# A hybrid decoder layer on 8 cores: query heads transposed in pairs, the convolution's projection ahead of the output transposes, and another order of the first transfers

## What is computed

```python
x = x + 0.5 * swiglu(rmsnorm(x, ffn1_norm), ffn1_w_gate, ffn1_w_up, ffn1_w_down)   # 1024 -> 2816 -> 1024
h = rmsnorm(x, mix_norm)
proj = h @ w_in            # q_lat 384 | kv_lat 256 | k_rope 32 | xc, gB, gC 1024 each | two gates 1024 each
q = (rmsnorm(q_lat, q_a_norm) @ w_uq).reshape(b, s, 8, 96)     # 64 plain dims, 32 rotary dims per head
c_kv = rmsnorm(kv_lat, kv_a_norm); k_nope = c_kv @ w_uk; v = c_kv @ w_uv
q, k = rmsnorm(q, q_head_norm), rmsnorm(k, k_head_norm)        # per head, then rotary on the last 32 dims
y_a = causal_block_attention(q, k, v) @ w_proj_attn
u = gC * xc
y_b = (gB * conv3(u)) @ w_proj_conv                            # causal, depthwise, width 3
x = x + (sigmoid(gA) * y_a + sigmoid(gB_) * y_b) @ w_out
x = x + 0.5 * swiglu(rmsnorm(x, ffn2_norm), ffn2_w_gate, ffn2_w_up, ffn2_w_down)
```

## Time and profile before

| | |
|---|---|
| time before, median of 3 runs | 3396.72 us (3071.61 to 3548.67) |
| the profiled execution, its own time | 3073.66 us |
| its span, slowest core | 3072.0 us (all cores 3068.7 to 3072.0) |
| mean granted TensorE clock of that core | 0.998 |
| VectorE busy | 1412.9 us (46%) |
| ScalarE busy | 1278.6 us (42%) |
| DMA | mean 147 GB/s, the weights' queue 82.7% of 16 engines' span |
| matmuls | 16807 |

### The profile page before, as it was taken

The page is one execution under the profiler, slowest core; times in us unless marked ns, Lnnn a source line. Parts: engine busy times, 40 slices in busy tenths (PEclk is TensorE's granted clock), DMA queues, the critical chain, the costliest instruction groups (busy, mean ns, idle before and its releaser), DMA issues.

```text
span 3072.0 us, 49838 instructions; the slowest of 8 cores (3068.7 to 3072.0 us)
## 1 busy us (share of the span) xinstructions
PE 3042.8 (99%) x16807; PEld 1442.3 (47%) x16807; DVE 1412.9 (46%) x2781; ACT 1278.6 (42%) x1983; POOL 384.1 (13%) x725
## 2 busy tenths in 40 slices
PE   8999999999999999999999999999999999999999
PEld 3444444444445444454444444444444544445544
DVE  4355554552545525455244552545425454254441
ACT  2244353631447314493143431446225562255730
POOL 1110110011100111001110011101111001110010
PEclk9999999999999999999999999999999999999999
DMA  9997898798986989859897998888988969878597
GB/s 175 162 151 128 145 148 156 140 167 139 151 166 123 156 141 146 158 96 161 146 158 140 161 164 144 136 169 141 166 141 132 180 113 166 144 130 155 86 156 147
DMA packets 122935, 451.87 MB, mean 147 GB/s; under 512 B 13888, under 2 KB 15040, under 8 KB 122560
## 3 DMA queue, kind: packets, MB, share of 16 engines
q0 software_dynamic: 103824, 414.82, 82.7%
q1 hardware_dynamic: 18864, 33.85, 3.7%
HBM read 846.62 MB, written 16.78 MB: 281 GB/s over the span
## 4 chain that ended last, share of the span: by engine, by line
PE 97%; DMA 2%; ACT 0%; DVE 0%; issue 0%; SPq 0%; DVEq 0%; ACTq 0%; POOLq 0%
PE bank L651 39%; PE bank L724 20%; PE bank L972 10%; PE bank L951 7%; PE bank L1026 4%; PE bank L1140 4%; PE bank L1121 4%; PE bank L752 2%; PE bank L1068 2%; PE bank L1126 2%; DMA ring<-ws 1%; PE bank L817 1%; PE bank L902 0%; PE bank L812 0%; PE bank L821 0%; PE bank L615 0%
## 5 line engine op out<-in xcount | busy, mean ns | idle before, releaser
L651 PE MATMUL bank<-hT,ring 128*128 128x512 bf16 x4768 | 1051.0, 380 | 9.8 <-DMA ring<-ws 7.5
L651 PEld LDWEIGHTS bank<-hT,ring 128*128 128x128 bf16 x4768 | 464.1, 98 | 567.5 <-issue 18.6
L533 POOL DMA_DIRECT2D ring<-ws x720 | 383.3, 535 | 2661.6 <-PE bank L651 959.6
L724 PE MATMUL bank<-actT,ring 128*128 128x512 bf16 x2816 | 615.6, 379 | 0.2 <-DMA ring<-ws 0.2
L1030 ACT ACTIVATE actT<-bank,negM,par_sb 128x512 bf16<-128x512 f32 (+3 forms) x640 | 424.4, 724 | 155.4 <-PE bank L1026 113.9
L658 DVE TENSOR_TENSOR actT<-sg,bank 128x512 bf16<-128x512 f32 x340 | 233.5, 687 | 550.7 <-PE bank L651 435.0
L657 ACT ACTIVATE sg<-bank 128x512 f32<-128x512 f32 x340 | 203.1, 597 | 587.9 <-PE bank L651 528.7
L724 PEld LDWEIGHTS bank<-actT,ring 128*128 128x128 bf16 x2816 | 274.0, 98 | 325.2 <-issue 0.7
L972 PE MATMUL bank<-hT,ring 128*128 128x512 bf16 x1344 | 379.5, 380 | 2.8 <-DMA ring<-ws 2.8
L727 DVE SCALAR_TENSOR_TENSOR xres<-bank,xres 128x512 f32<-128x512 f32 x128 | 88.5, 692 | 324.4 <-PE bank L724 324.4
L1026 PE MATMUL bank<-QT,KT 96*128 96x512 bf16 (+3 forms) x640 | 220.8, 349 | 0.0
(11 more groups left out here) (150 smaller groups left out, 2414.5 us busy)
## 6 DMA issues: line engine op xcount, KB each, us to landing
ring<-ws POOLq DMA_DIRECT2D x352, 512.0 KB, 8.8
ring<-ws POOLq DMA_DIRECT2D x128, 704.0 KB, 8.7
ring<-ws POOLq DMA_DIRECT2D x64, 896.0 KB, 10.6
ring<-ws POOLq DMA_DIRECT2D x64, 768.0 KB, 11.6
ring<-ws POOLq DMA_DIRECT2D x104, 256.0 KB, 9.8
xres<-x SPq DMA_DIRECT2D x64, 256.0 KB, 17.4
out<-xres SPq DMA_DIRECT2D x64, 256.0 KB, 10.0
uqkv<-ws POOLq DMA_DIRECT2D x1, 1088.0 KB, 19.0
```

The costliest lines, as they stand in the source:

```text
L533: [lambda e, off=off, wo_=wo_, F=F: e.dma_start(out=ring[:, off:off + F], in_=ws_d[:, wo_:wo_ + F])],
L651: op("pe", lambda e, k=k, a_=a_, wv=wv, pb=pb: e.matmul(pb[:], lhsT=wv[:, a_, k, :], rhs=h_[:, k, :], start=(k == 0), stop=(k == 7)), read ...
L724: op("pe", lambda e, kc=kc, wv=wv, ab=ab: e.matmul(ab[:], lhsT=wv[:, kc, :], rhs=actT[:, kc, :], start=(kc == 0), stop=(kc == NFC - 1)), r ...
```

## The change

Three edits.

**Queries.** The rows of `qf` change from 8 heads of 96 to 512 plain columns (8 x 64) followed by 256 rotary columns (8 x 32). Each of 6 transposes takes 128 columns: four hold two heads' plain dims, two hold four heads' rotary dims. The result is taken out of its bank in six operations: ScalarE the even heads' plain dims with the gain, VectorE the odd heads' with the gain, and four VectorE copies of the rotary rows. A second dependency `d_QTo` stands beside `d_QT` wherever QT is read or overwritten.

**Output.** In the first output chunk of a mixer `attn_tr()` moves from in front of the convolution's projection to behind it.

**Start.** POOL no longer issues a piece at once: it waits for x chunk 1 and then fills the ring. The rest of `par` and the positions leave the start of SP's queue: SP issues them when VectorE has written `actT` chunk 3, and the five small VectorE operations that follow from them run behind gate/up chunk 7.

```diff
@@ t_tr
-            for h in range(NH):
-                op("pe", lambda e, h=h: e.transpose(out=tqv[0:96, h, :], in_=qf[:, h, :], identity=identb[:]),
-                   reads=[d_qf, d_id], writes=[d_tq], signal=(h == NH - 1))
-            op("dve", lambda e: e.tensor_scalar(out=QT[0:96, :, tsl], in0=tqv[0:96, :, :],
-                                                 scalar1=par[0:96, P_GQC:P_GQC + 1], scalar2=None, op0=ALU.mult),
+            for a in range(6):
+                op("pe", lambda e, a=a: e.transpose(out=tqv[:, a, :], in_=qf[:, a * 128:(a + 1) * 128], identity=identb[:]),
+                   reads=[d_qf, d_id], writes=[d_tq], signal=(a == 5))
+            qd = QT[:, :, tsl].rearrange("p (a b) s -> p a b s", b=2)
+            qr = QT[:, :, tsl].rearrange("p (a b) s -> p a b s", b=4)
+            op("act", lambda e: e.activation(out=qd[0:64, :, 0, :], in_=tqv[0:64, 0:4, :], func=AF.Copy,
+                                              scale=par[0:64, P_GQC:P_GQC + 1]),
                reads=[d_tq, d_par, d_gqc], writes=[d_QT[tt]])
+            op("dve", lambda e: e.tensor_scalar(out=qd[0:64, :, 1, :], in0=tqv[64:128, 0:4, :],
+                                                 scalar1=par[64:128, P_GQC:P_GQC + 1], scalar2=None, op0=ALU.mult),
+               reads=[d_tq, d_par, d_gqc], writes=[d_QTo[tt]])
+            for i in range(4):
+                op("dve", lambda e, i=i: e.tensor_copy(out=qr[64:96, :, i, :], in_=tqv[i * 32:(i + 1) * 32, 4:6, :]),
+                   reads=[d_tq], writes=[d_QTo[tt]])
@@ mixer
-            if c == 0:
-                attn_tr()
             op("act", lambda e, b=b, c=c, pgb=pgb: e.activation(out=sbb[b][:], in_=pgb[:], func=AF.Sigmoid,
...
+            if c == 0:
+                attn_tr()
             pya, dpya = psum(MB)
@@ start
-    fw.dma("sp", s_set, [lambda e: e.dma_start(out=par[:, P_GQH:NPAR], in_=par_d[:, P_GQH:NPAR]),
-                         lambda e: e.dma_start(out=pos_t[:], in_=pos_d[:, :])], writes=[d_par[0], d_pos])
...
-        w_fill(1)
-        fw.wait("pool", [d_x[0][2]])
-        w_fill(2)
-        fw.wait("pool", [d_x[0][6]])
+        fw.wait("pool", [d_x[0][1]])
         w_fill()
...
+    def load_params():
+        fw.wait("sp", [d_act[3]])
+        fw.dma("sp", s_set, [lambda e: e.dma_start(out=par[:, P_GQH:NPAR], in_=par_d[:, P_GQH:NPAR]),
+                             lambda e: e.dma_start(out=pos_t[:], in_=pos_d[:, :])], writes=[d_par[0], d_pos])
...
+            sched[4] = [load_params] + sched.get(4, [])
-            for n, t in ((8, angles), (9, L(reduce_angle, 0.0)), (11, L(sine, sinT, d_sin)),
+            for n, t in ((7, late_params), (8, angles), (9, L(reduce_angle, 0.0)), (11, L(sine, sinT, d_sin)),
```

More of the change, by code:

```diff
@@ L317, in pack_params @@
     par[:, P_GKC] = 1.0
-    par[0:64, P_GQC] = np.asarray(inp["q_head_norm"], f32)[0:64]
-    par[0:64, P_GKC] = np.asarray(inp["k_head_norm"], f32)[0:64]
+    for i in (0, 64):
+        par[i:i + 64, P_GQC] = np.asarray(inp["q_head_norm"], f32)[0:64]
+        par[i:i + 64, P_GKC] = np.asarray(inp["k_head_norm"], f32)[0:64]
     return par
@@ L377, in build_program @@
     d_QT = [Dep(f"QT{t}") for t in range(TPG)]
+    d_QTo = [Dep(f"QTo{t}") for t in range(TPG)]
     attn_tok = sb("attn_tok", [128, TPG, 512], BF16)
@@ L450, in build_program @@
     d_qr = [d_atok[0]]
-    qf = atok_f[:, 512:1280].rearrange("p (h d) -> p h d", h=NH)
+    qf = atok_f[:, 512:1280]
+    qfn = qf[:, 0:512].rearrange("p (h d) -> p h d", h=NH)
+    qfr = qf[:, 512:768].rearrange("p (h d) -> p h d", h=NH)
     d_qf = [d_atok[1], d_atok[2]]
@@ L480, in build_program @@
     tA, tB, tC, tI = [QT_f[:, i * 1024:(i + 1) * 1024].bitcast(F32) for i in range(4)]
-    d_tA, d_tB, d_tC, d_tI = [[Dep(f"tt{i}")] + d_QT for i in range(4)]
+    d_tA, d_tB, d_tC, d_tI = [[Dep(f"tt{i}")] + d_QT + d_QTo for i in range(4)]
     tA = tA.rearrange("p (t f) -> p t f", f=16)
@@ L640, in norm_apply @@
                                                     op0=ALU.mult, op1=ALU.mult),
-           reads=[d_x[xb][c], d_rbc, d_par], writes=d_dst)
+           reads=[d_x[xb][c], d_rbc, d_parg], writes=d_dst)
     FB, AB = (0, 1, 2, 3), (4, 5, 6, 7)
@@ L858, in t_q @@
             sinb = sinT[:, gt_, None, :].broadcast_to([128, NH, 16])
-            rope(qf[:, :, 64:80], qf[:, :, 80:96], qr_t[:, :, 0:16], qr_t[:, :, 16:32], cosb, sinb,
+            rope(qfr[:, :, 0:16], qfr[:, :, 16:32], qr_t[:, :, 0:16], qr_t[:, :, 16:32], cosb, sinb,
                  [t.rearrange("p (h d) -> p h d", h=NH) for t in rt], d_rt, [d_qr, d_cos, d_sin], [d_qf])
@@ L865, in t_k @@
                 pv_ = pq[:, 0:384].rearrange("p (h d) -> p h d", h=4)
-                op("dve", lambda e, pv_=pv_, o=o: e.tensor_tensor(out=qf[:, o:o + 4, 0:64], in0=pv_[:, :, 0:64],
+                op("dve", lambda e, pv_=pv_, o=o: e.tensor_tensor(out=qfn[:, o:o + 4, :], in0=pv_[:, :, 0:64],
                                                                   in1=rhl[:, o:o + 4, None].broadcast_to([128, 4, 64]),
@@ L1027, in emit_S @@
                                         start=True, stop=True),
-               reads=[d_KT[kt], d_KTo[kt], d_KTr[kt]] + d_QT[jmin:], writes=[dps])
+               reads=[d_KT[kt], d_KTo[kt], d_KTr[kt]] + d_QT[jmin:] + d_QTo[jmin:], writes=[dps])
             pb = si % 4
@@ L1133, in mixer @@
             op("dve", lambda e, b=b, c=c: e.tensor_tensor(out=mrgT[:, c, :], in0=m1[b][:], in1=m2[b][:], op=ALU.add),
-               reads=[d_m1[b], d_m2[b]], writes=[d_mrg[c]] + (d_QT if c == 0 else []))
+               reads=[d_m1[b], d_m2[b]], writes=[d_mrg[c]] + (d_QT + d_QTo if c == 0 else []))
             for t in side_m4.get(c, ()):
@@ L1140, in wo_mm @@
                 op("pe", lambda e, k=k: e.matmul(po[:], lhsT=wv[:, k, :], rhs=mrgT[:, k, :], start=(k == 0), stop=(k == 7)),
-                   reads=[dw, d_mrg[k]] + (d_QT if c == 7 and k == 7 else []), writes=[dpo], signal=(k == 7))
+                   reads=[dw, d_mrg[k]] + (d_QT + d_QTo if c == 7 and k == 7 else []), writes=[dpo], signal=(k == 7))
         def wo_ev(c, po, dpo):
@@ L1202, in build_program @@
             norm_add(c - 1)
[L1203 to L1208, removed]
     TWO_PI = 2.0 * math.pi
@@ L1211, in build_program, with late_params @@
     C2 = TWO_PI - C1
+    def load_params():
+        fw.wait("sp", [d_act[3]])
+        fw.dma("sp", s_set, [lambda e: e.dma_start(out=par[:, P_GQH:NPAR], in_=par_d[:, P_GQH:NPAR]),
+                             lambda e: e.dma_start(out=pos_t[:], in_=pos_d[:, :])], writes=[d_par[0], d_pos])
+    def late_params():
+        op("dve", lambda e: e.tensor_copy(out=identb[:], in_=par[:, P_ID:P_ID + 128]), reads=[d_par], writes=[d_id])
+        op("dve", lambda e: e.tensor_copy(out=trib[:], in_=par[:, P_TRI:P_TRI + 128]), reads=[d_par], writes=[d_tri])
+        op("dve", lambda e: e.memset(negM[:], -SM_SHIFT), writes=[d_negM])
+        op("dve", lambda e: e.tensor_tensor(out=par[:, P_GQC:P_GQC + 1], in0=par[:, P_GQC:P_GQC + 1], in1=par[:, P_GKC:P_GKC + 1],
+                                             op=ALU.mult), reads=[d_par], writes=[d_gqc])
+        op("dve", lambda e: e.tensor_copy(out=posf[:], in_=pos_t[:]), reads=[d_pos], writes=[d_posf])
     def angles():
```

## The result

Both kernels were run in turn, 20 executions each. In some executions of either kernel the cores of one die or of both show a lower granted clock and a longer time, and these are left out. The comparison of the others, called undisturbed, gives a ratio of 1.0017 (95% interval 1.001 to 1.0025) against the kernel before, with medians of 3077.8 and 3072.5 us: **5.3 us slower**, small but clearly outside the noise. The forecast of 3072.6 us said no change.

What follows compares the result with a forecast made beforehand. TensorE, busy 99% of the span, was taken as the bound. Query transposes -3.6, order at the end of attention +4.5 and start -2.0 summed to -1.1 us, from 3073.66 to 3072.6 us, range 3063 to 3084.

Steps and rivals of the forecast that it cites:

- rival (c): At the start: x chunk 1 lands as late as before, 10.2 us after issue; 3077.5 us, chance 0.10.
- Part 1: Query transposes: two fewer in each of 32 tiles, 3.6 us less on TensorE; between -3.6 and -0.6.
- I cost the eviction at nothing: Query transposes: the longer eviction is hidden and adds no time, with +3 us as its end.
- rival (e): Query transposes: the longer eviction holds a bank, +3 to 7 us, 3076 to 3080; chance 0.08.
- Part 2: End of attention: waits before the transposes give way to 1.8 us before attention's projection; +4.5 us over 8 stages.
- TensorE is free at 327.99: End of attention, first mixer: the moved projection starts then and ends at 329.72, so transposes start at once.
- The rival by which the order pays as written: End of attention: the 9.1 us of waits go and no other comes; 3059 us, chance 0.06.
- the one by which the new wait slows the clock: Before attention's projection: the clock falls, 1.7 us a stage, 13.7 in all 8, so 3086 us; chance 0.12.
- Part 3: The start: TensorE gets 3.4 us ahead, but transfers gain only 2.1; 2.0 us less, between 0 and 4.7.
- its 0.26 MB take 0.9 us: The start: x chunk 1, issued at 1.98 us, transfers in 0.9 us and lands near 5.7.
- 3.4 us ahead: The start: the first 24 gate/up matmuls end at 22.7 us where they ended at 26.09 before.
- the one in which the start pays in full: The start: the transfers follow, so -4.7 instead of -2.0 us; 3070 us, chance 0.17.

Runs made afterwards that it cites:

- e3: Label not defined in the text; third run told: the start edit alone against the kernel before, ratio 1.0004 (0.9993 to 1.0014).
- e10: Label not defined in the text; by context a run splitting the start against the kernel before: POOL's single wait, 3070.74 us, or parameters moved, 3074.95 us.

## Why the prediction was right or wrong

The direction was wrong: −1.1 us was the sum, +5.3 us came. That the time lies within the range owes something to luck: the range was drawn for errors on either side, and the forecast itself had a chance of 0.47. By its number the time also fits rival (c), 3077.5, whose mechanism didn't occur.

**Part 1: wrong.** The count and price of the transposes hold: 192, and six in 0.34 us are 0.056 us each. The step that failed is "I cost the eviction at nothing". I made the new eviction 1.6 us long and let ScalarE's copy run beside it. The timeline of the first tile of after, core 5, shows what it is:

```profile
205.55 0.68 ACT L910 ACTIVATE QT<-bank,par_sb 64x512 bf16<-64x512 bf16 x1 [3.08 <-PE bank L906]
...
206.34 0.49 DVE L913 TENSOR_SCALAR QT<-bank,par_sb 64x512 bf16<-64x512 bf16 x1 [2.15 <-ACT QT L910]
...
206.93 1.46 DVE L917 COPY QT<-bank 32x256 bf16<-32x256 bf16 x4
```

The kernel marks each bank so that its readers on different engines follow one another in program order. So L913 could start only when L910 was done, 0.79 us after L910 had started. (The 2.15 us in the bracket is all of VectorE's idle time, most of it from before the transposes.) The time of a copy was right:

```profile
L917 DVE COPY QT<-bank 32x256 bf16<-32x256 bf16 x128 | 36.9, 288 | 13.9 <-DVE QT L917 0.9
```

Each takes 0.288 us where I had drawn a line to 0.29, but 0.10 us of waiting stands before each of the four. From the start of ScalarE's copy to the end of the last copy it is 206.93 + 1.46 − 205.55 = 2.8 us: my 1.6, and 0.8 for ScalarE's copy, and 0.4 for the four pauses. My margin of 1.4 us became a wait of 0.11 in two tiles of each group. No run took away the order of the readers or the pauses alone, so what each is worth by itself isn't shown. And "for the last tile of a group only the mixer follows" left out what is queued behind the copies on VectorE: the last residual, which the first scores wait for in front of the mixer. That is the wait L1038 of the list. The experiments with the earlier transposes show both, since the full 0.45 us per group comes back when the eviction starts sooner. The rival (e), the longer eviction holds a bank, had the mechanism at a chance of 0.08 and +3 to 7 us; with the residual's queue it came to 1.8 + 2.7 = 4.5.

**Part 2: right, with a term too large.** The waits, their number and their size (1.6 us, 13 us together) came as worked, and the price nearly so (+4.5, measured 4.2 in the changed kernel and 3.9 alone). Where the edit acts it was 3.5 and 3.4. The difference is the step "TensorE is free at 327.99": that is the end of a value matmul with the tail in which the next can already run. In the changed kernel the last value matmul starts at 329.10 and the projection at 329.12, so each of the eight old waits was really 0.16 us longer than the profile has it (9.1 us in sum), and filling them gave back 8 x 0.16 = 1.3 us more: 4.7 − 1.3 = 3.4. The rival by which the order pays as written is refuted. So is the one by which the new wait slows the clock. The window behind the wait of the first mixer (columns as above):

```profile
334.00:336.00 2.00, 2.00 (x11) 0.93 (x10) 1.22 (x2) 0.00 (x0) 0.53 (x1) 1.00 0.04 7
```

The granted clock is 1.00, after 1.64 us without work, and on none of the eight cores does a fall of the clock lie behind one of the 64 such waits. The Trainium skill (TensorE: Matmul & The Clock Gate, Part 1) has the throttled state as the default; that did not show after pauses of this length.

**Part 3: wrong in its middle.** The order of events came as told, the times did not. POOL issued its pieces at 8.56 us, not 6.2, and the first gate/up matmul came at 16.56 on core 5, 15.7 to 18.7 over all cores, not at 15.6:

```profile
8.56 3.84 POOL L537 DMA_DIRECT2D ring<-ws  x7 [7.87 <-DMA xres<-x]
...
16.56 7.50 PE L655 MATMUL bank<-hT,ring 128*128 128x512 bf16 x24 [7.54 <-DMA ring<-ws]
```

The step that failed is "its 0.26 MB take 0.9 us": I let chunk 1 pass as if it were alone. By 8.0 us SP's queue had moved 0.97 MB:

```profile
q1 hardware_dynamic: 665, 0.97, 58.4%
```

Chunks 0 and 1 and the first parameters are 0.54 MB of it. Seven chunks were issued within 3.5 us, and 0.43 MB of the later ones had moved before chunk 1 was there. The rate was lower than forecast as well: 0.97 MB in the 5.8 us from the first packet at 2.2 us, where I had taken 0.56 MB in 2 us. Either alone would still have given 5.4 to 5.7 us. And piece 0 was not the only reason why chunk 1 was late before: without it the chunk was taken up at 8.0 us instead of 12.1, not at 5.7. A second step failed with it: "Before they ended at 26.09", so "3.4 us ahead", was read from core 3, the slowest and, at this point, the latest of the eight. The norm's matmuls stood at 21.5 to 25.9 us before, 23.3 on the mean; after, at 24.1. TensorE was not 3.4 us ahead at this point but level: eight other profiled kernels with the start of before have means of 23.6 to 24.3. The first down matmul came 0.2 us later where 2.0 earlier was forecast. The waits that were to grow in front of it did not: from 27 to 110 us TensorE waited 1.6 us on the mean of the cores, 2.0 before. Whether the packets ran faster, as the 2.1 us of the prediction has it, no run shows. The rival "x chunk 1 lands as late as before" is refuted in its size (8.0, not 12.2), and the one in which the start pays in full is refuted by e3, e10 and the changed kernel alike.

**The sum again**, with what was measured: Part 1 +0.9, Part 2 +4.2, Part 3 about 0: +5.1, of 5.3.

## What to carry to other kernels

An eviction that is split over two engines and into small pieces is as long as its parts in a row where the kernel orders the readers of a bank, as this one does; count it to its end, pauses between the pieces too, and ask what is queued behind it on each engine. Work used as cover in front of one wait is taken from the wait behind it: write the stretch as the larger of wait and cover, plus the fixed part, before moving anything. Cover is free only if it needs no new buffer, and if TensorE was the bound where it came from. Read a start from all cores, since the slowest core of one execution is partly chance.

## What the runs showed of the hardware that I had not expected

- VectorE's copies of 32x256 bf16 out of a bank took 0.288 us each, two thirds of the 0.426 us of a 64x512 one, which has four times the elements; and 0.10 us passed between one copy and the next that waits for it, where 0.03 us passed before the multiply (L662) that doesn't. ScalarE's of 64x512 with a scale took 0.68 us, more than VectorE's 0.49 for the same shape.
- After 1.64 us without work TensorE kept the full clock, and after 2.56 us the next 2 us had 0.54.
- Of seven chunks issued together on one queue, the first landed 6 us after its issue, when 0.97 MB had moved; what stood ahead of it and itself are 0.54 MB, 2 us at the rate of the earlier trace rows.
